# Norms of the delta rule's heads: twelve 256-column products into rows in place of twenty-four one-column products

## The reference

```python
def l2_norm(x):
    xf = x.astype(jnp.float32)
    return (xf * lax.rsqrt(jnp.sum(xf * xf, axis=-1, keepdims=True) + EPS)).astype(x.dtype)

def gated_deltanet(qkv, gate, b_raw, a_raw, conv_w, A_log, dt_bias, out_gain):
    qkv = jax.nn.silu(causal_depthwise_conv(qkv, conv_w))
    q, k, v = (t.reshape(b, s, A_HEADS, A_HEAD_DIM) for t in jnp.split(qkv, 3, axis=-1))
    q = l2_norm(q) * A_HEAD_DIM ** -0.5
    k = l2_norm(k)
```

## Time and profile before

| | us |
|---|---|
| median of three executions | 1201.66 |
| the profiled execution | 1201.49 |
| its span in the profile | 1199.3 |
| TensorE busy (matmul) | 1191.1 |
| VectorE busy | 934.9 |
| ScalarE busy | 730.3 |
| GpSimd busy | 91.0 |

### The profile page before, as it was taken

The page is one execution under the profiler, slowest core; times in us unless marked ns, Lnnn a source line. Parts: engine busy times, 40 slices in busy tenths (PEclk is TensorE's granted clock), DMA queues, the critical chain, the costliest instruction groups (busy, mean ns, idle before and its releaser), DMA issues.

```text
span 1199.3 us, 22399 instructions
## 1 busy us (share of the span) xinstructions
PE 1191.1 (99%) x7956; PEld 1097.4 (92%) x7956; DVE 934.9 (78%) x1612; ACT 730.3 (61%) x1211; POOL 91.0 (8%) x105
## 2 busy tenths in 40 slices
PE   9999999999999999999999999999999999999998
PEld 9899999888888999999888889988888999888887
DVE  7666788988876789788988767888876777888853
ACT  7554656666664589467666645666654566666642
POOL 5850000000000001610000000000000000000000
PEclk9999999999999999999999999999999999999999
DMA  8544655555564344115555743555664323555730
GB/s 327 181 143 167 208 201 190 195 183 205 206 238 154 140 168 166 64 36 173 194 194 184 262 160 121 203 193 178 225 233 148 134 104 118 199 202 183 252 134 36
DMA packets 48143, 209.92 MB, mean 175 GB/s; under 512 B 3486, under 2 KB 4908, under 8 KB 43596
## 3 DMA queue, kind: packets, MB, share of 16 engines
q1 hardware_dynamic: 46720, 204.96, 48.4%
q10 hardware_dynamic: 1356, 4.07, 1.0%
HBM read 207.90 MB, written 1.13 MB: 174 GB/s over the span
## 4 chain that ended last, share of the span: by engine, by line
PE 93%; DVE 4%; ACT 1%; issue 1%; DMA 1%; DVEq 0%; SPq 0%; ACTq 0%
PE main L2141 25%; PE main L2143 13%; PE main L2461 13%; PE main L2114 8%; PE main L2115 8%; PE main L2116 8%; PE main L2463 7%; DVE w_lo L1141 1%; PE side L2247 1%; PE main L2620 1%; PE main L2504 1%; PE side L2221 1%; PE side L2504 1%; PE main L2795 1%; PE main L2797 1%
## 5 line engine op out<-in xcount | busy, mean ns | idle before, releaser
L1141 DVE TENSOR_TENSOR w_lo<-raw,w_hi 128x1024 fp32r<-128x1024 f32 (+3 forms) x365 | 468.8, 1292 | 7.5 <-ACT w_hi L579 6.4
L2141 PE MATMUL main<-xs,w_hi 128*128 128x512 f32 x1328 | 461.1, 390 | 0.6 <-DVE xs L1175 0.6
L579 ACT ACTIVATE w_hi<-raw 128x1024 fp32r<-128x1024 f32 (+2 forms) x363 | 402.3, 1110 | 70.3 <-PE main L2116 50.1
L2143 PE MATMUL main<-xs,w_lo 128*128 128x256 f32 x1328 | 374.5, 282 | 0.0
L2141 PEld LDWEIGHTS main<-xs,w_hi 128*128 128x128 f32 x1328 | 249.2, 188 | 53.3 <-DVE xs L1175 0.9
L2143 PEld LDWEIGHTS main<-xs,w_lo 128*128 128x128 f32 x1328 | 251.0, 189 | 0.0
L2461 PE MATMUL main<-h_both,w_hi 128*128 128x512 f32 x682 | 236.6, 390 | 0.0
L2463 PE MATMUL main<-h_both,w_lo 128*128 128x256 f32 x682 | 192.3, 282 | 0.0
L2461 PEld LDWEIGHTS main<-h_both,w_hi 128*128 128x128 f32 x682 | 128.0, 188 | 26.8
L2463 PEld LDWEIGHTS main<-h_both,w_lo 128*128 128x128 f32 x682 | 128.9, 189 | 0.0
L2114 PE MATMUL main<-xs,w_hi 128*128 128x256 f32 x368 | 105.4, 287 | 0.0
(11 more groups left out here) (488 smaller groups left out, 1915.1 us busy)
## 6 DMA issues: line engine op xcount, KB each, us to landing
raw<-in_w_gu_a SPq DMA_DIRECT2D x44, 1024.0 KB, 5.2
raw<-in_w_gu_b SPq DMA_DIRECT2D x44, 1024.0 KB, 5.2
raw<-in_w_down_a SPq DMA_DIRECT2D x16, 1408.0 KB, 6.1
raw<-in_w_down_b SPq DMA_DIRECT2D x16, 1408.0 KB, 5.9
raw<-in_w_in SPq DMA_DIRECT2D x15, 1024.0 KB, 5.6
raw<-in_w_in_a SPq DMA_DIRECT2D x13, 1024.0 KB, 5.1
raw<-in_w_gates SPq DMA_DIRECT2D x4, 1024.0 KB, 5.2
raw<-in_w_up SPq DMA_DIRECT2D x4, 1024.0 KB, 5.2
```

Source lines behind the costliest of these rows:

```text
L579: act.activation(w_hi[:, u % RING, 0:n], raw[:, s % RAW, u % 2, 0:n], ACT.Copy).then_inc(hi_ready, 1)
L1141: return dve.tensor_tensor(dst, src, hi.bitcast(F32), ALU.subtract)
L2141: pe.matmul(bank[:, :], piece(w_hi, u, k), xs[:, k], start=k == 0, stop=k == KC - 1, skip_group_check=True)
L2143: ins = pe.matmul(bank[:, 0:SEQ], piece(w_lo, u, k), xs_hi[:, k], start=False, stop=k == KC - 1, skip_group_check=True)
```

## The change

The selector pick is a strip of eleven columns, 128x11, zero but for its sixth column, which is one. It is set at the start by VectorE with two memsets. The six columns 5-m to 10-m of it (m = n mod 6) are a 128x6 matrix with ones in column m. This becomes the stationary side, and the squares of a head, all 256 tokens at once, the moving side: the sums of head m go to row m of a 6x256 result and zeros are added to the other rows. Six products accumulate in one group, so the result holds six heads as rows.

VectorE copies the rows from PSUM to SBUF at t=9 (keys) and t=15 (queries), into free partitions of sp1 and sp2. TensorE turns them at t=11 and t=17 with two float32 products each against a 6x6 identity, into columns 256 to 267 of the same side bank. VectorE reads the columns from there at t=12 as before, and at t=17 in place of t=16. Its waits for csum move to the copies; the readings wait for rows_t instead. ba_dve and ba_t are renamed rows_dve and rows_t, since they count the new events as well.

```diff
+        sum_rows = [sp1[0:6, :], sp2[0:6, :]]
...
+        pick = small[:, 50:61]
...
+            link(dve.memset(pick, 0.0))
+            link(dve.memset(pick[:, 5:6], 1.0))
...
                 if t == 12:
 
-                    dve.wait_ge(csum, 6)
-                    dve.tensor_scalar(sums[:, :, 0:6], side[3][:, 0:12].rearrange("p (c h) -> p c h", c=2), EPS, None,
+                    dve.wait_ge(rows_t, 2)
+                    dve.tensor_scalar(sums[:, :, 0:6], side[3][:, SEQ:SEQ + 12].rearrange("p (c h) -> p c h", c=2), EPS, None,
                                       ALU.add).then_inc(sums_ready, 1)
...
-                if t == 16:
-
-                    dve.wait_ge(csum, 12)
+                if t in (9, 15):
+                    j = (t - 9) // 6
+                    dve.wait_ge(csum, 6 * (j + 1))
+                    dve.tensor_copy(sum_rows[j], (side[3], side[0])[j][0:6, 0:SEQ]).then_inc(rows_dve, 1)
+                if t == 17:
+
+                    dve.wait_ge(rows_t, 3)
                     dve.wait_ge(col_act, 1)
-                    dve.tensor_scalar(sums[:, :, 6:12], side[0][:, 0:12].rearrange("p (c h) -> p c h", c=2), EPS, None,
+                    dve.tensor_scalar(sums[:, :, 6:12], side[0][:, SEQ:SEQ + 12].rearrange("p (c h) -> p c h", c=2), EPS, None,
                                       ALU.add).then_inc(sums_ready, 1)
...
                     for n in (t - 5, t - 4):
                         sums_to = side[3] if n < 6 else side[0]
                         pe.wait_ge(csq_ready, n + 1)
-                        for c in range(2):
-                            ins = pe.matmul(sums_to[:, c * 6 + n % 6:c * 6 + n % 6 + 1],
-                                            csq[:, n % 4, c * P:(c + 1) * P], ones[:, 0:1], start=True, stop=True)
-                        ins.then_inc(csum, 1)
+                        pe.matmul(sums_to[0:6, 0:SEQ], pick[:, 5 - n % 6:11 - n % 6], csq[:, n % 4, :], start=n % 6 == 0,
+                                  stop=n % 6 == 5).then_inc(csum, 1)
+                if t in (11, 17):
+                    j = (t - 11) // 6
+                    pe.wait_ge(rows_dve, 3 + j)
+                    for c in range(2):
+                        ins = pe.matmul((side[3], side[0])[j][:, SEQ + 6 * c:SEQ + 6 * (c + 1)],
+                                        sum_rows[j][:, c * P:(c + 1) * P], ident[0:6, 0:6], start=True, stop=True)
+                    ins.then_inc(rows_t, 1)
```

More of the change, by code:

```diff
@@ L387, in program @@
         gate_silu, tap_done = sem("gate_silu"), sem("tap_done")
-        ba_act, ba_dve, ba_t, col_act = (sem(n) for n in ("ba_act", "ba_dve", "ba_t", "col_act"))
+        ba_act, rows_dve, rows_t, col_act = (sem(n) for n in ("ba_act", "rows_dve", "rows_t", "col_act"))
         gram, decay_ready, n_ready, a_masked = (
@@ L886, in _ @@
                     act.activation(ba[0:6, :], ba[0:6, :], ACT.Exp, scale=-1.0).then_inc(ba_act, 1)
-                    act.wait_ge(ba_dve, 1)
+                    act.wait_ge(rows_dve, 1)
                     link(act.activation(sp2[32:38, :], sp1[32:38, :], ACT.Abs))
@@ L894, in _ @@
                 if t == 7:
-                    act.wait_ge(ba_dve, 2)
+                    act.wait_ge(rows_dve, 2)
                     act.dma_start(delta_rows, ba[32:38, :]).then_inc(rows_out, 16)
@@ L1619, in _ @@
                     dve.tensor_scalar(sp1[32:38, :], ba[32:38, :], par[32:38, C_DT:C_DT + 1], None, ALU.add)\
-                       .then_inc(ba_dve, 1)
+                       .then_inc(rows_dve, 1)
                 unit_done(u0 + t)
@@ L1645, in _ @@
                                                      ALU.mult, ALU.add)
-                    ins.then_inc(ba_dve, 1)
+                    ins.then_inc(rows_dve, 1)
                 if t == 11:
-                    dve.wait_ge(ba_t, 1)
+                    dve.wait_ge(rows_t, 1)
                     link(dve.tensor_copy(cols[:, 0:76], side[2][:, 0:76]))
@@ L2534, in _ @@
                         pe.wait_ge(csq_ready, n + 1)
-                        for c in range(2):
-                            ins = pe.matmul(sums_to[:, c * 6 + n % 6:c * 6 + n % 6 + 1],
-                                            csq[:, n % 4, c * P:(c + 1) * P], ones[:, 0:1], start=True, stop=True)
-                        ins.then_inc(csum, 1)
+                        pe.matmul(sums_to[0:6, 0:SEQ], pick[:, 5 - n % 6:11 - n % 6], csq[:, n % 4, :], start=n % 6 == 0,
[7 more added lines that the diff above has]
+                    ins.then_inc(rows_t, 1)
                 if t == 10:
-                    pe.wait_ge(ba_dve, 2)
+                    pe.wait_ge(rows_dve, 2)
                     for c in range(2):
@@ L2543, in _ @@
                                            ident[0:38, 0:38])
-                    ins.then_inc(ba_t, 1)
+                    ins.then_inc(rows_t, 1)
                 if t == 13:
```

## The result

The changed kernel takes 1203.99 us (median of 15, 1203.10 to 1204.35) against 1201.65 for the kernel before (15 runs, 1201.35 to 1201.92), 2.34 us more; the ratio is 1.0019, 95% interval 1.0012 to 1.0026. The forecast was 1203.0 in a range of 1202.0 to 1204.5. The direction and the class (within 0.2%) came out, the size did not: +2.3 in place of +1.3.

A forecast was written before the change was run, and what follows sets the result against it. TensorE, busy 1191.1 of 1199.3 us, was taken as the bound; -0.09 at t=9, +0.21 for three groups and +1.20 for two turns gave +1.3 us, so 1203.0 us, range 1202.0 to 1204.5.

The forecast's parts named there:

- the rival that emptied the array: Each selector group and turn: every change of form empties the array, 1.16 per group, 0.8 per turn, +2.9, 1204.5; chance 0.16.
- TensorE is the bound, one for one behind 434.56: Projections stage: before 434.56 TensorE's gains are lost waiting for a square; afterwards its gains or losses move the end fully.
- The floor that I named through sums_ready, +0.65: Third grams at t=19: the second sums, ready near 469.5, set a floor of about +0.65 under any saving.
- The removed products: Six groups of one-column float32 products: 0.894 us each, 0.11 per pass for loading 128-column weights; 1.20 at t=9 with its wait.
- The added passes: Each new selector group: two float32 products of 256 moving columns, four passes at 0.217, 0.867 us streaming.
- The change of form: Selector groups among projections: 0.10 on entry, nothing on exit, so +0.07 each at t=11, 13 and 15.
- The turns: At t=11 and t=17, turning six rows into columns: 0.6 us each, between 0.4 and 0.8, 1.20 in all.
- The wait at t=9: Group at t=9, waiting for the second square ready at 434.56: ends at 435.03 in place of 435.12, a gain of 0.09.
- VectorE's copies: Two 6x256 copies at t=9 and t=15, about 0.4 each: nothing late, a margin of 0.25 before TensorE asks at t=11.

The follow-up runs named there:

- cols_t10: Kernel before with its t=9 group of one-column products moved to t=10, nothing else; 1201.72 us, ratio 0.9998.
- r_cols: Kernel before with squares and ones in fp32r, two moving columns of ones, nothing turned; 1201.65 us, ratio 0.9999.
- r_full: Changed kernel with fp32r squares and a 128-column fp32r selector, copies and float32 turns on all 128 rows; 1202.98 us, ratio 1.0008.
- wide_pick: Changed kernel with the selector 128 columns wide in place of 6, the added rows zero and not read; 1203.05 us, ratio 1.0014.
- r_pick: Changed kernel with squares and selector in fp32r, the form still 128*6; 1202.62 us, ratio 1.0007.
- r_cols_t10: Kernel before with fp32r squares and ones and its t=9 group moved to t=10; 1201.77 us, ratio 1.0002.
- all_full: Changed kernel with a 128-column selector, and copies and turns on all 128 rows too; 1202.55 us, ratio 1.0008.
- pick32: Changed kernel with the selector 32 columns wide in place of 6, the added rows zero and not read; 1203.96 us, ratio 1.0020.

## Why the prediction was right and wrong

The range held the result, but the interval given to the forecast itself (1202.6 to 1203.5) did not: the measured time lies between the forecast and the rival that emptied the array, and it was for that rival that the range went up to 1204.5.

- **TensorE is the bound, one for one behind 434.56.** Right for losses: the stage's 2.52 stands undiminished at the end. Wrong for gains: cols_t10, r_cols. The floor that I named through sums_ready, +0.65, is of the right size: in the changed kernel VectorE's reading ends at 468.44, about 0.6 us behind the place, counted from the start of the stage, at which TensorE's loads of t=19 stand in the kernel before. r_full ran into it, with VectorE 0.7 us later still. In the kernels without copies and turns the wait that bound was n_ready, and it had no margin in the kernel before.
- **The removed products**, 0.894 a group: right, and r_cols halved it by halving the passes (0.45 a group). That the load of the 128 weight columns sets the 0.11 of a pass fits this, but no run varied the load alone.
- **The added passes**, 0.867 for four: right (0.86 in wide_pick, 1.156 less entry and exit in the changed kernel).
- **The change of form**: the step that failed, a term that was sized too small. I took 0.10 on entry from L2360 and nothing on exit. Measured: 0.09 and 0.20. L2360 is followed by other float32 products of one column and not by a projection, so I read only its start from the row, and booked the exit at zero without a reason. Six groups at +0.26 in place of +0.07 are 1.15 us, nearly all of the miss. The rival that emptied the array had it: 1.16 a group by its reckoning, 1.156 measured. It was too wide in saying this of every change of form: r_pick's costs nothing. Its turns, 0.8 each, were too dear (0.53 and 0.73), hence its +2.9.
- **The turns**, 0.6 each: the sum is right, 1.26 against 1.20, in part by luck: one was 0.07 too dear and the other 0.13 too cheap. What I had counted as one price depends on what stands ahead of the turn.
- **The wait at t=9**: a gain of 0.09 was forecast there; with the dearer groups TensorE came late enough not to wait, and the 0.31 were used up in full (from t=5 to behind t=9 TensorE lost about 0.5 in all).
- **VectorE's copies**: hidden, as forecast. In the changed kernel's timeline of DVE the first copy ends at 441.04 and the turn starts at 442.03, a distance of 1.0 where I had a margin of 0.25; the second set of sums is read at 468.28 and the third grams start at 470.50.

```profile
440.63 0.41 DVE L1672 COPY sp<-side 6x256 f32<-6x256 f32 x1
...
459.51 0.41 DVE L1672 COPY sp<-side 6x256 f32<-6x256 f32 x1
...
468.28 0.16 DVE L1677 TENSOR_SCALAR cols<-side 128x12 f32<-128x12 f32 x1
```

## What to carry to other kernels

Here a group of small float32 products among full-width products paid 0.3 us for leaving the full form, once per group; try to pad its weights with zeros to 128 columns (or its rows to 128) before you count columns saved, or give it fp32r (shown here for few weight columns, not for few rows). When a price is read off a neighbour, check that the row shows both its sides; a side that it can't show is unknown, not zero. And before buying time on the busiest engine, look at how far ahead of it the others are: here under 0.1 us at t=20. And each wait of 1.3 us or more on TensorE in this stage was paid twice, once as a wait and once in clock.

## What the runs showed of the hardware that was not expected

The granted clock fell to 0.5 for about three microseconds behind single waits of 1.3, 1.5, 1.9 and 2.4 us in the midst of dense products (r_cols_t10, r_cols, r_pick, r_full), and waits of 0.4 (all_full, wide_pick) and 0.8 (before) left it alone.

One VectorE operation, the split of weights near 53 us, takes 3.34 us in some executions and 1.43 in others, also where the program text up to there is the same (pick32 has the long one, wide_pick the short one). Kernel before, then changed kernel:

```profile
52.91 3.34 DVE L1141 TENSOR_TENSOR w_lo<-raw,w_hi 128x1024 fp32r<-128x1024 f32 x1
```

```profile
53.26 1.43 DVE L1143 TENSOR_TENSOR w_lo<-raw,w_hi 128x1024 fp32r<-128x1024 f32 x1
```

Behind the short one everything stands 1.0 us earlier: that is the 0.69 above (0.35 behind, then 1.04 ahead). Of the thirteen profiles, eight have the long one and five the short one, in no visible relation to the edit. It touches the medians little: of the changed kernel's 15 executions only the profiled one has a span of 1201.2, the others have 1201.8 to 1202.2. What holds the operation is not in the trace and stays open. It is as large as a forecast's error here, and the reason that the stage and not the span was compared.
